# Moving a block substitution to GpSimd and an attention norm behind the recurrence's first output, in a hybrid RWKV-7 / forgetting-attention / expert layer

## What is computed

```python
h = rms_norm(x, attn_norm_g[l])
u = h @ w_in[l]
y_rwkv = rwkv7_group(u[..., :RWKV_IN], ...)   # 8 heads of 64: a recurrence over tokens
y_fox = fox_group(u[..., RWKV_IN:], ...)      # 8 heads of 64: causal attention with forget gates
mix = jnp.concatenate([y_rwkv, y_fox], axis=-1)
x = x + mix @ w_out[l]
x = x + moe_ffn(rms_norm(x, ffn_norm_g[l]), ...)   # top 4 of 32 experts
```

## Time and profile before

| | |
|---|---|
| median of 3 runs | 1628.32 us (1628.27 to 1628.34) |
| the profiled execution | 1627.85 us, its span 1626.1 us |
| busy share of the span | PE 96%, DVE 82%, ACT 63%, POOL 36% |
| mean granted PE clock | 0.987 of full speed |

### The profile page before, as it was taken

The page is one execution under the profiler, slowest core; times in us unless marked ns, Lnnn a source line. Parts: engine busy times, 40 slices in busy tenths (PEclk is TensorE's granted clock), DMA queues, the critical chain, the costliest instruction groups (busy, mean ns, idle before and its releaser), DMA issues.

```text
span 1626.1 us, 23302 instructions
## 1 busy us (share of the span) xinstructions
PE 1558.0 (96%) x7924; PEld 1273.9 (78%) x7924; DVE 1337.4 (82%) x1175; ACT 1019.4 (63%) x881; POOL 584.1 (36%) x397
## 2 busy tenths in 40 slices
PE   6999989899999999999999999999999999999994
PEld 5777778795577788888888888888888888888883
DVE  4499766433688899999999999999999999999894
ACT  4534233420366677777777777777777777777774
POOL 5633611332231114434333434333334432343431
PEclk9999999999999999999999999999999999999997
DMA  5322011111579999999999999999999999999994
GB/s 175 129 81 78 14 15 53 53 53 35 181 264 314 390 374 376 378 384 382 381 381 384 374 375 384 386 375 382 380 367 393 381 377 378 382 385 376 385 379 158
DMA packets 146771, 467.15 MB, mean 287 GB/s; under 512 B 21046, under 2 KB 35036, under 8 KB 146716
## 3 DMA queue, kind: packets, MB, share of 16 engines
q1 hardware_dynamic: 136908, 437.37, 71.1%
q0 software_dynamic: 9664, 28.53, 7.5%
q10 hardware_dynamic: 144, 0.52, 0.1%
HBM read 443.67 MB, written 22.71 MB: 287 GB/s over the span
## 4 chain that ended last, share of the span: by engine, by line
PE 77%; DVE 11%; DMA 6%; ACT 2%; issue 2%; SPq 0%; POOL 0%; DVEq 0%; POOLq 0%; ACTq 0%
PE banks L1704 19%; PE banks L1706 19%; PE banks L1705 19%; DMA slots<-in_expert_w_dram 5%; PE banks L1649 3%; DVE lo L2059 2%; PE banks L1713 2%; PE banks L1733 1%; PE banks L1536 1%; PE banks L1352 1%; PE banks L1353 1%; PE banks L1354 1%; PE banks L1699 1%; PE banks L1546 1%; ACT hi L1136 1%
## 5 line engine op out<-in xcount | busy, mean ns | idle before, releaser
L2059 DVE TENSOR_TENSOR lo<-slots,hi 128x2048 fp32r<-128x2048 f32 x384 | 863.7, 2284 | 47.5 <-PE banks L1706 24.7
L1136 ACT CAST hi<-slots 128x2048 fp32r<-128x2048 f32 x384 | 734.8, 1914 | 255.8 <-DMA slots<-in_expert_w_dram 210.5
L1704 PE MATMUL banks<-lo,x_hi 128*128 128x512 f32 x1040 | 412.1, 396 | 0.4 <-DVE lo L2059 0.4
L1706 PE MATMUL banks<-hi,x_lo 128*128 128x512 f32 x1040 | 407.6, 392 | 0.0
L1705 PE MATMUL banks<-hi,x_hi 128*128 128x512 f32 x1040 | 407.0, 391 | 0.0
L918 POOL DMA_INDIRECT x_sum<-hT,idy x32 | 90.2, 2820 | 494.3 <-ACT hT L1224 479.5
L1706 PEld LDWEIGHTS banks<-hi,x_lo 128*128 128x128 f32 x1040 | 196.1, 189 | 41.8
L1704 PEld LDWEIGHTS banks<-lo,x_hi 128*128 128x128 f32 x1040 | 196.4, 189 | 40.1 <-DVE lo L2059 0.6
L1705 PEld LDWEIGHTS banks<-hi,x_hi 128*128 128x128 f32 x1040 | 196.4, 189 | 39.8
L1704 PE MATMUL banks<-lo,a_hi 128*128 128x512 f32 x496 | 195.2, 394 | 3.9 <-DVE lo L2059 3.8
L1706 PE MATMUL banks<-hi,a_lo 128*128 128x512 f32 x496 | 193.8, 391 | 0.0
(11 more groups left out here) (375 smaller groups left out, 1960.8 us busy)
## 6 DMA issues: line engine op xcount, KB each, us to landing
slots<-in_expert_w_dram SPq DMA_DIRECT2D x384, 1024.0 KB, 12.0
slots<-in_w_in_dram SPq DMA_DIRECT2D x13, 1024.0 KB, 5.3
xs<-in_x_dram SPq DMA_DIRECT2D x8, 512.0 KB, 5.8
slots<-in_w_out_dram SPq DMA_DIRECT2D x2, 2048.0 KB, 7.9
x_sum<-xs SPq DMA_DIRECT2D x4, 512.0 KB, 9.5
h_rows<-slots SPq DMA_DIRECT2D x4, 512.0 KB, 2.6
xs<-x_sum SPq DMA_DIRECT2D x4, 512.0 KB, 5.0
x_sum<-xs POOLq DMA_DIRECT2D x3, 512.0 KB, 10.6
```

The source lines that it names most:

```text
L1136: nc.scalar.copy(w_hi[n % HI][:, :, :], raw[r]).then_inc(hi_ready, 1)
L1704: nc.tensor.matmul(out, x_h, w_l, start=first, stop=False)
L1706: return nc.tensor.matmul(out, x_l, w_h, start=False, stop=last)
L2059: tensor_tensor(w_lo[n % LO][:, :, :], raw[n % RAW], w_hi[n % HI][:, :, :], ALU.subtract).then_inc(lo_ready, 1)
```

## The change

1. The second half's substitution goes from DVE to POOL: a function `substitute(f, s)`, called for f = 1 at fox steps 7 to 14 of POOL's stream. The semaphore `identity_set` goes.
2. `finish_fox` ends after the scaling. The squares and their sums (`fox_squares`) come two steps later, at the turn of steps 11, 19 and 27; those of the last block in a stage `frms`.
3. The attention has 34 steps in place of 39, so the 36 inversion stages lie in 30 steps in place of 35. Roots, scaling and transposes are stages `frms`, `fscale`, `foT` inside the recurrence: the roots at its start, the rest behind the first Y. The transposes go to PSUM banks 6 and 7.

The experts' code is the same.

```diff
-        FOX_NORM = len(units) + 2
-        FOX_STEPS = FOX_NORM + TT + 1
+        FOX_STEPS = len(units) + 2
...
+        for at, st in ((2, ("frms", 0)), (15, ("fscale", 0)), (17, ("fscale", 1)), (19, ("foT", 0)), (21, ("fscale", 2)),
+                       (23, ("foT", 1)), (25, ("fscale", 3)), (27, ("foT", 2)), (30, ("foT", 3))):
+            recurrence.insert(at, st)
+        assert recurrence.index(("Y", 0)) < recurrence.index(("foT", 0)) < recurrence.index(("foT", TT - 1)) < recurrence.index(("yT", 0))
+        rwkv_stages += recurrence
...
+            elif kind == "foT":
+                put(st, 6 + tt % 2)
...
+            def substitute(f, s):
+                rest = dprod[:, f, 0:s * (DB - s)].rearrange("p (r c) -> p r c", r=s)
+                shape = [P, s, DB - s]
+                step(nc.gpsimd.tensor_tensor(rest, dblock[:, f, 0:s, s:s + 1].to_broadcast(shape),
+                                             dinv[:, f, s:s + 1, s:].to_broadcast(shape), ALU.mult))
+                step(nc.gpsimd.tensor_tensor(dinv[:, f, 0:s, s:], dinv[:, f, 0:s, s:], rest, ALU.subtract))
+                if s == 1:
+                    pool.sem_inc(diag_inverted[f], 1)
...
+                if kind == "fox" and 7 <= tt < 7 + DB // 2:
+                    if tt == 7:
+                        pool.wait_ge(diag_read[1], 16)
+                    for s in range(DB - 1 - 2 * (tt - 7), max(DB - 3 - 2 * (tt - 7), 0), -1):
+                        substitute(1, s)
...
+                if kind == "frms":
+                    fox_rms(act)
+                    continue
+                if kind == "foT":
+                    fox_out_T(act, tt)
+                    continue
...
+
+            def fox_squares(qb):
+                f = heads_of(fo[:, qb, :])
                 dve.wait_ge(fox_o_free, qb + 1)
...
                 if i > H and i % H == 1:
                     finish_fox(i // H - 1)
-                if FOX_NORM <= i < FOX_NORM + TT:
-                    scale_fox(i - FOX_NORM)
+                if i > H and i % H == 3:
+                    fox_squares(i // H - 1)
...
                 if kind == "fox":
                     fox_step(tt)
-                    if 6 <= tt < 6 + DB // 2:
-                        invert_blocks(tt - 6)
+                    continue
+                if kind == "frms":
+                    fox_squares(TT - 1)
+                    continue
+                if kind == "fscale":
+                    scale_fox(tt)
                     continue
```

More of the change, by code:

```diff
@@ L347, in hymba_layer @@
         xt_cleared = sem("xt_cleared")
-        identity_set = sem("identity_set")
         l_moved = sem("l_moved")
@@ L501, in hymba_layer @@
         rwkv_stages += between(fox_stages[FOX_ALONE:], by_halves((0, 1)))
-        rwkv_stages += between(inversion((2, 3)),
-                               prepare(0) + [("MV", 0), ("U", 0), ("Yfrom", 0), ("state", 0), ("Y", 0)]
-                               + prepare(1) + [("MV", 1), ("U", 1), ("yT", 0), ("Yfrom", 1), ("state", 1), ("Y", 1)]
-                               + prepare(2))
+        recurrence = between(inversion((2, 3)),
+                             prepare(0) + [("MV", 0), ("U", 0), ("Yfrom", 0), ("state", 0), ("Y", 0)]
+                             + prepare(1) + [("MV", 1), ("U", 1), ("yT", 0), ("Yfrom", 1), ("state", 1), ("Y", 1)]
+                             + prepare(2))
+        for at, st in ((2, ("frms", 0)), (15, ("fscale", 0)), (17, ("fscale", 1)), (19, ("foT", 0)), (21, ("fscale", 2)),
[3 more added lines that the diff above has]
+        rwkv_stages += recurrence
         rwkv_stages += [("MV", 2)] + between(prepare(3), [("U", 2), ("Yfrom", 2), ("state", 2), ("yT", 1), ("Y", 2)])
@@ L532, in hymba_layer @@
                     put(("PT", *units[tt - 1]), 2)
-                if tt > FOX_NORM:
-                    put(("foT", tt - FOX_NORM - 1), 2)
             elif kind in ("X0", "P", "X", "XT") and tt < 2:
@@ L549, in hymba_layer @@
                 nth_of["p"] += 1
-            elif kind not in ("Y", "x0"):
+            elif kind not in ("Y", "x0", "frms", "fscale"):
                 put(st, nth_of["r"] % 6)
@@ L810, in _ @@
             select(dinv, [[0, 2], [1, DB], [-1, DB]], ALU.not_equal, 1.0, 0, 0)
-            pool.sem_inc(identity_set, 1)
             step(nc.gpsimd.memset(zero_i, 0))
@@ L826, in _ @@
                 w_in_low_part(n)
+            def substitute(f, s):
[6 more added lines that the diff above has]
+                    pool.sem_inc(diag_inverted[f], 1)
             pool.wait_ge(diag_read[0], 16)
             for s in range(DB - 1, 0, -1):
-                rest = dprod[:, 0, 0:s * (DB - s)].rearrange("p (r c) -> p r c", r=s)
-                shape = [P, s, DB - s]
-                step(nc.gpsimd.tensor_tensor(rest, dblock[:, 0, 0:s, s:s + 1].to_broadcast(shape),
-                                             dinv[:, 0, s:s + 1, s:].to_broadcast(shape), ALU.mult))
-                step(nc.gpsimd.tensor_tensor(dinv[:, 0, 0:s, s:], dinv[:, 0, 0:s, s:], rest, ALU.subtract))
-            pool.sem_inc(diag_inverted[0], 1)
+                substitute(0, s)
             pool.wait_ge(elem_done, JT)
@@ L971, in fox_out_T @@
             for j in range(JT):
-                ins = nc.scalar.mul(hT[:, JT + j, qb * P:(qb + 1) * P], bank[2][:, j * P:(j + 1) * P], vec("og", j))
+                ins = nc.scalar.mul(hT[:, JT + j, qb * P:(qb + 1) * P], bank[6 + qb % 2][:, j * P:(j + 1) * P], vec("og", j))
             ins.then_inc(free_of(("foT", qb)), 1)
@@ L1113, in fox_step @@
                     exponentials(i)
-                if i == FOX_NORM:
-                    fox_rms(act)
             def fox_turn(i):
@@ L1119, in fox_turn @@
                     exponentials(i + 1)
-                if i > FOX_NORM:
-                    fox_out_T(act, i - FOX_NORM - 1)
             def move(name, dst, src):
@@ L1467, in fox_turn @@
                     values(i - 2)
-                if i > FOX_NORM:
-                    fo_transposes(i - FOX_NORM - 1)
             heads = [(h, h // 2, (h % 2) * N) for h in range(H)]
@@ L1520, in _ @@
                     v_transposes(tt)
+                    continue
+                if kind == "foT":
+                    fo_transposes(tt)
                     continue
@@ L2101, in _ @@
             tensor_tensor(rw[:, :, :], rw[:, :, :], vec("g2").unsqueeze(2).to_broadcast([P, KT, E]), ALU.mult).then_inc(rw_ready, 1)
-            def invert_blocks(part):
-                if part == 0:
-                    dve.wait_ge(identity_set, 1)
-                    dve.wait_ge(diag_read[1], 16)
-                for s in range(DB - 1 - 2 * part, max(DB - 3 - 2 * part, 0), -1):
-                    rest = dprod[:, 1, 0:s * (DB - s)].rearrange("p (r c) -> p r c", r=s)
-                    shape = [P, s, DB - s]
-                    step(tensor_tensor(rest, dblock[:, 1, 0:s, s:s + 1].to_broadcast(shape),
-                                       dinv[:, 1, s:s + 1, s:].to_broadcast(shape), ALU.mult))
-                    step(tensor_tensor(dinv[:, 1, 0:s, s:], dinv[:, 1, 0:s, s:], rest, ALU.subtract))
-                if part == DB // 2 - 1:
-                    dve.sem_inc(diag_inverted[1], 1)
             for st in rwkv_stages:
```

## The result

| | before | after |
|---|---|---|
| median, first comparison, 12 runs each | 1628.37 us | 1618.72 us (1614.76 to 1625.96) |
| ratio, 95% interval | | 0.9936 [0.9924, 0.9947] |
| ratio, second comparison, another chip | | 0.9955 [0.9939, 0.9971] |
| profiled execution, its span | 1627.85, 1626.1 | 1614.76, 1613.0 |
| first scores to the first product group of chunk 1 | 117.77 us | 106.21 us |

The first ratio is 10.4 us [8.6, 12.4], the second 7.3 us [4.7, 9.9]. Forecast were 10.7 us and 1617.6: the change is faster (neither interval reaches 1), by about what was forecast or a little less.

The account below looks back on a forecast made before the run. DVE's queue and lost clock bound attention steps 8 to 15, PE steps 16 to 33, the norm's chain the tail. Terms sum to -10.7 us: 1627.85 becomes 1617.2, plus 0.5 for the median, 1617.6 us; range 1614.0 to 1624.0.

Parts of the forecast that it names:

- four pairs: Attention steps 8 to 15: without the substitution on DVE, 4.3 us a pair of units where it was 5.5, -4.9 us.
- the pair before: Pair ahead of unit 8: PE's 0.82 us idle, when DVE's copy stands behind a substitution, goes, -0.8 us.
- denser list, later squares: Steps 16 to 33: 2.7 us of inversion stages no longer hidden, less DVE waits that later squares mostly remove, net +1.5 us.
- tail: Between the attention's last values and the recurrence's first stage: PE no longer waits for the norm, -11.0 us.
- norm behind Y: In the recurrence: four transposes, 1.8 us, and a PE wait of 2.7 us for DVE behind the first Y, +4.5 us.
- POOL late: At X0 of half 1: POOL's half ready near 227.8, `xt_in[1]` near 237, needed about 238.6; slack 1.6 us, cost 0.
- the one clean pair: Pair of unit 14 in the kernel before, without substitution on DVE: 3.9 us, the base for pricing the pairs.
- the idle also costs clock: Attention, behind PE's 2.71 us idle before 224.80: granted clock 0.56 and 0.59, mostly the lower of two levels.
- Rival 1: Attention pairs stay held by scores, maxima, exponentials, transposes and copy at 5.0 us each: -6.7 us, 1621.6 us; chance 0.22.
- Rival 3: POOL's operations at twice DVE's time, 0.5 us: `xt_in[1]` 2.2 us late for PE, 1619.8 us; chance 0.10.
- Rival 4: POOL's operations at about 0.8 us: half 1 late, PE waits 11.8 us at X0, clock 3.4 more, 1632.8 us; chance 0.04.
- Rival 2: Clock falls behind the new 2.7 us idle behind the first Y, losing 3.4 us: 1621.0 us; chance 0.14.

Follow-up runs that it names:

- the squares back: Changed kernel with the squares of the first three blocks put back in `finish_fox`, behind the scaling; ratio to before 0.9928 from four runs.
- the added operations: Changed kernel with half 1's multiplication issued two or three times on POOL, 15 or 30 operations more; one time each, 1622.67 and 1629.46 us.
- the change again: The changed kernel, unchanged, run and profiled a second time on another chip; ratio to before 0.9955, 1616.57 us beside 1624.05.
- the substitution back: Changed kernel with half 1's substitution put back on DVE; later squares, denser list and moved norm stay; ratio to before 0.9987.
- the substitution alone: Kernel before with only half 1's substitution moved from DVE to POOL, run twice; ratios to before 0.9983 and 0.9979.
- the gap filled: Changed kernel with the norm's scaling ahead of Y on DVE and its last two transposes moved before a waiting KAR product group; ratio to before 0.9914.

## Why the prediction was right

By its own steps, each against the two first profiles:

| term | forecast | measured |
|---|---|---|
| four pairs | -4.9 | -5.62 (22.13 to 16.51) |
| the pair before | -0.8 | -1.06 (16.61 to 15.55, from the first scores to unit 8) |
| denser list, later squares | +1.5 | +1.8 |
| tail | -11.0 | -11.0 |
| norm behind Y | +4.5 | +4.36 |
| POOL late | 0 | 0, slack 2.4 us |
| sum | -10.7 | -11.6 at the first KAR |

**The pairs** were priced from the one clean pair plus 0.4. A pair took 4.1 us, between that 3.9 and my 4.3: PE's own work at full clock, as said. The sentence that the idle also costs clock there holds, by the pair of unit 12 above. What the prediction had incomplete is what held the pairs before: it named DVE's queue and the clock, and not that three of DVE's operations stood 2.1 us behind POOL's level masks. The term came out because it was read from a pair with none of the three. Rival 1, that the chain of scores, maxima and copies holds a pair at 5 us, is refuted by the 16.4 to 16.5 us of every kernel that has the substitution on POOL and either the later squares or the old list (17.15 with the squares back).

**The denser list** and **the tail** came as worked out: 47.88 us from unit 16 to the recurrence's first stage, 46.1 to its last values before. The squares' share is confirmed by their own run: putting them back costs 1.7 us, 0.64 of it in the pairs. Without the later squares steps 16 to 33 would have cost 2.8 us (1.8 + 1.0), the 2.7 of the prediction.

**The norm** cost 4.36 us, of which 2.42 is the wait (forecast 2.7) and the rest transposes. The wait is one for DVE's order and not for data; taking it away gave 2.62 us at the stage. The other three transposes had no wait, as forecast.

**POOL.** Half 1 was ready 0.3 us earlier than forecast. The slack is 2.4 us and not 1.6, mainly because the path from POOL's last operation to X0 takes 8.0 us; I had used 9. The operations came 0.36 us apart on average, close to the 0.37 of the earlier trace rows, so the rule of the Trainium skill that speaks against the move did not hold here: "GPSIMD Engine Reference" gives 2x for two inputs, the traces of before and after have 0.39 against 0.26 at 63 and 64 columns, 1.5 times. By that rule the prediction had PE wait 2.2 us at X0, and it waited nothing. Rival 3 falls. Rival 4's mechanism is shown by the added operations, with a wait of 7.42 and 2.0 us of clock behind it, where I had set 3.4 for the clock behind a wait of 11.8. Its premise fell: the operation that I had in view (0.66 us) appears once and not thirty times.

**Rival 2**, the clock behind the new wait, was told as an alternative with a chance of 0.14 and a price of 3.4 us. It is neither: the clock fell behind this wait in three of the six profiles that have it (the change again, the squares back, the substitution back), at 1.4 to 1.7 us each. So it belongs in the sum with half of 1.5 us. The old tail has the same lottery at its 3.39 us wait, where one of the four profiles that have it fell, the first of the substitution alone (40.33 us from unit 24 to the recurrence's transposes, and 38.83 in the three others).

**The end.** The forecast of 1617.6 stands 1.1 us below the measured median, which is well inside the range of 1614 to 1624, and inside the first interval (-10.7 against -10.4 [-12.4, -8.6]). By the second comparison (-7.3 [-9.9, -4.7]) it was 0.8 us outside. The sum at the first KAR was 0.9 us larger than forecast, and the end on average 2 us smaller; between these two stands the part of the program in which executions differ by more than that, and I can't assign the difference. So the terms are confirmed one by one at the first KAR; that the end agrees to about 1 us in the first comparison is finer than either comparison can tell, and in part luck.

## What to carry to other kernels

When an engine's queue, and not its busy share, sets the pace of a stage, move the work that nobody waits for out of it or behind what somebody waits for. Then look at each new wait: if the operation waited for stands behind others that it doesn't need, put it ahead of them, here worth 2.6 us more, and lay loose work of the bound engine into the waits that remain (0.9 us).

Look also at what the moved operations collide with: an operation that takes several times its usual time, and ends with one of another engine, is a cost of the place and not of the work. Two stages of equal length can have different causes, so compare their waits before one cause is ruled out.

Before an engine is given more work off the critical path, work out its slack by the latest moment at which the result is needed, and measure it by adding work until a wait appears. A single profile is one draw from several: compare a stage that the change touches across profiles, and the end by many runs.

## What the runs showed of the hardware

**The same wait, two clocks.** In twelve profiles the granted clock fell behind a given wait in some and not in others, though order and length of the wait were equal: 0.85 us near 206 (it fell in the change again and with the substitution back), 2.42 us behind Y (three of six), 1.97 us at the last chunk's products. Nor does the length alone tell: in the pairs it fell around the 2.7 us wait of both profiles of before, and not around the waits of 1.93 and 2.17 us with the substitution back. There PE's timeline has, in the profile of after and in the one with the gap filled:

```profile
365.65 1.97 PE L1617 MATMUL banks<-slots 128*128 128x64 f32 x16 [1.97 <-issue]
```

```profile
362.68 3.64 PE L1619 MATMUL banks<-slots 128*128 128x64 f32 x16 [1.97 <-issue]
```

Four profiles have the 1.97 us for the sixteen products, eight 2.6 to 3.7. The falls near 206 and behind Y cost 1.25 to 1.65 us each, those in the sixteen products 0.6 to 1.7 there. They are a part of the 11 us by which twelve runs of one kernel differ; another is in the experts, which take 1158.4 to 1163.0 us from their first product to the end of the span in the twelve profiles, the two profiles of the change at the low end of it.

**A wait of 2.4 us that nobody ordered.** At the last token tile of the router, DVE's copy of the counts waits for PE's products alone. In nine of twelve profiles it starts some 2.4 us behind their modelled end, with "remote" in the place of a releaser; in three (one of before, one of the change, one of the substitution alone) it starts right behind it. With it the clock falls, and the stretch from the output projection to the experts takes 87.1 to 89.0 us instead of 82.6 to 83.7. It comes in the kernel before as in the changed ones, so it is no effect of the change. What it is stays open; no run was made on it.

**Two engines at one memory.** POOL's substitution operations of 60 to 64 columns take 0.30 to 0.32 us, except one in each of the seven profiles whose rows show them singly beside the squares: it takes 0.77 to 0.86. In the profile of after it starts at 221.72, and so do the squares on DVE:

```profile
221.72 0.68 DVE L2037 TENSOR_TENSOR slots<-slots 128x512 f32<-128x512 f32 x1
```

The squares have two inputs from SBUF. DVE's other operations in this stretch read one input from PSUM, and POOL's keep their pace beside them. The Trainium skill, in "SBUF — State Buffer" (Who interferes with whom, and the summary), describes this: an operation of VectorE with two inputs from SBUF and one of GpSimd that reads SBUF lock each other out, and the later one waits for the whole of the other. The trace agrees: POOL's operation ends 0.16 us behind the squares. Here it cost POOL 0.5 us out of its slack. The other way round it costs more: DVE's substitution operations, with two inputs from SBUF, took 0.53 to 1.34 us in place of 0.2 when they met a level mask on POOL (1.26 us).
